# The order of the first loads in a hybrid retention/SSD layer on eight cores

## What is computed

```
mod = silu(cond) @ w_ada + b_ada                 # shift, scale, gate, twice (6 x 1024)
h   = x * (1 + scale1) + shift1
q, k, v, g, z, [xs, B, C], dt = split(h @ w_in)  # 3592 columns
ret = bidirectional retention (4 heads, decay per head, swish gate, RMS norm)
ssd = bidirectional SSD (8 heads; depthwise conv of width 5 and silu on xs, B, C; gated RMS norm)
x   = LN1(ALPHA * x + gate1 * (concat(ret, ssd) @ w_out))
x   = LN2(ALPHA * x + gate2 * SwiGLU(x * (1 + scale2) + shift2))
```

## Time and profile before

| what | value |
|---|---|
| median of 3 runs | 834.82 us (832.24 to 897.93) |
| the profiled execution, its own time | 834.51 us |
| its span, first to last instruction, core 0 | 833.5 us (the 8 cores: 825.6 to 833.5) |
| TensorE matmul busy in the span | 706.9 us, 85% |
| DVE, ACT, POOL busy | 49%, 40%, 35% |
| mean granted TensorE clock, core 0 | 0.938 |

### The profile page before, as it was taken

How to read it: one execution, slowest core, us unless ns; L and a number is a source line. 1 busy time by engine, 2 the same in 40 slices (tenths; PEclk the granted TensorE clock), 3 DMA queues, 4 the chain that set the end, 5 groups by cost and what they waited for, 6 DMA issues and landing times.

```text
span 833.5 us, 12875 instructions; the slowest of 8 cores (825.6 to 833.5 us)
## 1 busy us (share of the span) xinstructions
PE 706.9 (85%) x4414; PEld 371.5 (45%) x4414; DVE 410.9 (49%) x655; ACT 334.9 (40%) x580; POOL 294.9 (35%) x239
## 2 busy tenths in 40 slices
PE   0335999999999986987958399999999999999991
PEld 0333455655565543545425144444444444444440
DVE  0223322544689999487797831112222221466574
ACT  0322334638765333668667261211111111234533
POOL 2012100036655736434945655020000000254555
PEclk9957999989999999998978699999999999999996
DMA  8999400607546376570100937187443336011111
GB/s 181 229 202 159 77 1 11 105 8 118 91 63 105 39 127 142 176 159 20 51 0 26 138 64 101 16 103 87 52 51 50 51 52 152 27 50 74 53 51 76
DMA packets 62431, 69.57 MB, mean 83 GB/s; under 512 B 6144, under 2 KB 52768, under 8 KB 62240
## 3 DMA queue, kind: packets, MB, share of 16 engines
q0 software_dynamic: 47920, 40.72, 35.3%
q1 hardware_dynamic: 14448, 28.03, 10.5%
HBM read 101.05 MB, written 8.40 MB: 131 GB/s over the span
## 4 chain that ended last, share of the span: by engine, by line
PE 69%; DVE 10%; DMA 9%; issue 8%; ACT 3%; POOL 1%; DVEq 0%; ACTq 0%; POOLq 0%
PE psum L450 68%; DVE arena L484 6%; DMA arena<-w_in 4%; DMA arena<-w_ada 4%; DVE arena L495 3%; ACT arena L464 3%; PE psum L515 1%; POOL arena L484 1%; DVE arena L491 1%; ACT L464 1%; DVE arena L499 0%; DVEq L329 0%; DVE arena L505 0%; POOL arena L509 0%; ACTq L329 0%
## 5 line engine op out<-in xcount | busy, mean ns | idle before, releaser
L450 PE MATMUL psum<-arena 128*128 128x512 bf16 (+6 forms) x4208 | 678.5, 320 | 91.0 <-DMA arena<-w_ada 48.7
L450 PEld LDWEIGHTS psum<-arena 128*128 128x128 bf16 (+2 forms) x4208 | 344.5, 101 | 418.8 <-issue 120.1
L484 POOL TENSOR_TENSOR arena<-arena 128x1024 f32<-128x1024 f32 (+3 forms) x156 | 239.9, 1555 | 223.9 <-ACT arena L464 136.7
L464 ACT ACTIVATE arena<-psum 128x512 bf16<-128x512 f32 (+1 forms) x200 | 114.5, 596 | 260.3 <-PE psum L450 244.7
L464 ACT ACTIVATE arena<-arena 128x1 f32<-128x1 f32 (+8 forms) x232 | 144.3, 639 | 150.3 <-DVE arena L495 87.8
L484 DVE TENSOR_TENSOR arena<-arena,psum 128x512 bf16<-128x512 bf16 (+2 forms) x126 | 91.9, 736 | 200.1 <-PE psum L450 178.0
L484 DVE TENSOR_TENSOR arena<-psum,arena 128x512 f32<-128x512 f32 (+3 forms) x174 | 109.3, 649 | 51.0 <-PE psum L450 43.8
L495 DVE SCALAR_TENSOR_TENSOR arena<-arena 128x512 f32<-128x512 f32 (+2 forms) x84 | 95.5, 1160 | 12.2 <-ACT arena L464 11.7
L464 ACT ACT_TABLE_LOAD x32 | 41.1, 1283 | 45.5 <-PE psum L450 24.5
L484 DVE TENSOR_TENSOR arena<-arena 128x1 f32<-128x1 f32 (+8 forms) x74 | 53.5, 730 | 9.3 <-ACT arena L464 5.6
L464 ACT ACTIVATE arena<-psum,arena 128x512 bf16<-128x512 f32 (+1 forms) x56 | 39.3, 717 | 36.0 <-PE psum L450 30.8
(11 more groups left out here) (14 smaller groups left out, 38.6 us busy)
## 6 DMA issues: line engine op xcount, KB each, us to landing
arena<-w_ada POOLq DMA_DIRECT2D x12, 1024.0 KB, 18.0
arena<-x SPq DMA_DIRECT2D x6, 1024.0 KB, 12.4
arena<-w_in POOLq DMA_DIRECT2D x6, 1024.0 KB, 14.4
arena<-x SPq DMA_DIRECT2D x12, 512.0 KB, 4.6
arena<-w_gate POOLq DMA_DIRECT2D x11, 512.0 KB, 7.7
arena<-w_up POOLq DMA_DIRECT2D x11, 512.0 KB, 8.6
y<-arena SPq DMA_DIRECT2D x11, 512.0 KB, 2.6
arena<-w_down POOLq DMA_DIRECT2D x5, 1024.0 KB, 10.4
```

The source lines that it names most:

```text
L450: return P.op(PE, lambda e: e.matmul(out, lhsT=lhsT, rhs=rhs, start=start, stop=stop), [lhsT, rhs], [out], c)
L464: return P.op(ACT, lambda e: e.activation(out=out, in_=in_, func=func, **kw), [in_] + [v_ for v_ in (bias, scale) if isap(v_)], [out] + ([ ...
L484: return P.op(veng(eng), lambda e: e.tensor_tensor(out=out, in0=in0, in1=in1, op=op), [in0, in1], [out], vcost(eng, out, [in0, in1]))
```

## The change

It orders the loads of the start anew. The four small constants (`cols`, the identity block, `smalls`, `tailpos`) get a priority above all else, so SP issues them ahead of x chunk 0. x chunks 1 and 2 no longer wait for the third and the fourth issued `w_ada` slot, but all four halves for the landing of `wBC`. `wxs` waits for the first half of chunk 2, and `tpos`, `cos_t` and `sin_t` wait for `wxs`. No operation is added or taken away.

```diff
+    P.prio = 1e4
     dma(SP, cols[:], cols_d[:, :], "c2")
     dma(SP, V(0, 384, F32), cf_d[:, 0:384], "c0")
     dma(SP, smalls[:], bcast_row(R_SMALL, 48), "c3")
     dma(SP, tailpos[:], cf_d[:, CF_TAIL:CF_TAIL + 2], "c7")
+    P.prio = 0.0
...
     wa = [(ft0, mod_load(ft0)) for ft0 in (0, 8, 4, 12)]
-    wa_ops = [o for o in P.ops if o.is_dma and o.eng == POOL]
     dma(POOL, V(1536, 256, BF16), cb_d[:, 0:256], "c1")
-    x_load(1, 0, after=wa_ops[2:3])
-    x_load(1, 1, after=wa_ops[2:3])
-    x_load(2, 0, after=wa_ops[3:4])
-    x_load(2, 1, after=wa_ops[3:4])
...
     wBC = w_slot(w_in_d, 3072, 520)
+    bc_op = P.ops[-1]
+    xl = [x_load(ck, half, after=[bc_op]) for ck in (1, 2) for half in range(2)]
...
-        dma(SP, tpos, cf_d[:, CF_DELTA:CF_DELTA + 384], "tpos")
+        dma(SP, tpos, cf_d[:, CF_DELTA:CF_DELTA + 384], "tpos", after=[xs_op])
...
-    wxs = w_slot(w_in_d, 2560)
+    wxs = w_slot(w_in_d, 2560, after=[xl[2]])
+    xs_op = P.ops[-1]
...
-    dma(SP, cos_t, cf_d[:, CF_COS:CF_COS + 1024], "c4")
-    dma(SP, sin_t, cf_d[:, CF_SIN:CF_SIN + 1024], "c5")
+    dma(SP, cos_t, cf_d[:, CF_COS:CF_COS + 1024], "c4", after=[xs_op])
+    dma(SP, sin_t, cf_d[:, CF_SIN:CF_SIN + 1024], "c5", after=[xs_op])
```

## The result

| | before | after |
|---|---|---|
| median of the runs, same chip | 833.97 us | 842.85 us |
| the profiled execution, its own time | 834.51 us | 842.82 us |
| its span | 833.5 us (core 0) | 841.8 us (core 2) |
| spans of the 8 cores | 825.6 to 833.5 us | 836.2 to 841.8 us |
| mean granted TensorE clock of the core shown | 0.938 | 0.933 |

The ratio is 1.0112 (95% interval 1.0085 to 1.014): 9 us slower, where 14 were forecast.

The account below looks back on a forecast made before the run. The prediction took the start, up to TensorE's dense stretch, to bound the kernel. It added 10.8 us for the stop, 2.5 for the clock and 0.7 for table loads, 14.0 in all, to 834.51: 848.5 us, range 838 to 856.

Parts of the forecast that it names:

- Small constants: 0: Start loads: small constants ahead of x chunk 0 don't reach the path, since TensorE first waits for a `w_ada` slot.
- `wBC` at 48.5 (47.5 to 50): POOL's queue: the B/C/dt weights land at 48.5 us, 28 us earlier than before.
- x last at 73.7, projections from 76.9: SP's queue and TensorE: late x takes back the 28 us gain; projections begin at 76.9 against 76.98.
- The stop: 10.8 of shift: First Silu on ACT: Exp waiting for late `tpos` hold it until 99.1, against 88.3 before; TensorE waits 10.6 us.
- the first way: Landing of `wxs`: summed from x's 18 us, the remaining bytes at 0.15 MB/us and 1 us for landing, 90.2.
- The clock: 2.5: TensorE after its stop: 13 matmuls at half speed, 2.5 us more, bounds 0 and 3.5.
- The other table loads: 0.7: ACT between Silu: eight more table loads mostly fit, costing TensorE 0.7 us, bounds 0 and 10.3.
- Rival (c): ACT between Silu: the table loads aren't hidden and add up, 858 us; chance 0.14.
- the stretches from 150 us on as before, 14 us later: Rest of the kernel: from 150 us everything runs as before, only 14 us later.
- (a): First Silu on ACT: the Exp don't hold ACT, `wxs` lands by 81.4, only x counts, 834 to 838; chance 0.11.
- (b): Start loads: early `wxs` and quick x make it faster, 831.5, or 830 with `wBC` at 47; chance 0.04.
- (d): TensorE at its stop: the clock stays up or data comes otherwise, 845 to 846; inside the range, no separate chance.

Follow-up runs that it names:

- const_first: Kernel before with only the four small constants issued ahead of x chunk 0, lists made anew; 835.72 us, ratio 0.9992.
- tpos_nowait: Changed kernel, same lists on every engine, only the wait of `tpos` for `wxs` left out; 838.09 us, ratio 1.0046.
- both_same_order: Changed kernel, same lists, without the waits of x chunks 1 and 2 for `wBC` and of `tpos` for `wxs`; 824.06 us, ratio 0.9872.
- wbc_first: Kernel before with `wBC` ahead of `wz` on POOL's queue, lists of TensorE, ACT and DVE kept; ratio 0.9878.
- both_early: Changed kernel without the waits of x chunks 1 and 2 for `wBC` and of `tpos` for `wxs`, scheduled anew; 820.36 us, ratio 0.9822.
- x_early_resched: Changed kernel with x chunks 1 and 2 issued at once, `tpos` still behind `wxs`, lists made anew; 819.83 us, ratio 0.9818.

## Why the prediction was right, and where its sum was off

The mechanism came as predicted: x takes back what `wBC` gains, ACT waits for `tpos` ahead of the first Silu, TensorE stops for ACT. Point by point:

**Small constants: 0.** Right; const_first alone is 0.9992.

**`wBC` at 48.5 (47.5 to 50).** It landed at 49.90, inside the bounds. The working was a little off: SP's queue was not empty at 16 us, it moved 1.70 MB from 2 to 16 and 0.68 after that, and POOL's queue had moved 0.85 MB by then, not 0.61.

**x last at 73.7, projections from 76.9.** The last piece was there at 75.98, inside the bounds (70.7 to 76.5); the projections began at 80.56. Of these 3.7 us 2.3 are the landing, most of it `wBC`'s 1.4. The rest is the transposes: those behind the last landing took 4.6 us, not 3.2, since the granted clock was 0.50 from 77.30 to 80.70, after TensorE had waited 3.00 for the piece: the 14 transposes at 77.55 took 3.22 us where 14 took 1.72 before. And I compared with core 0 of before, 76.98, a late one; the median of the cores is 75.6. Alone the late x is a loss of 3.8 us and not 0: that is tpos_nowait's 1.0046. In the change it is hidden behind the wait for `tpos`.

**The stop: 10.8 of shift.** Measured at the same Silu: 96.63 - 88.27 = 8.4. The step that failed is the landing of the two loads and one table load. `wxs` landed 2.0 earlier than the 92.2 that I chose between 90.2 and 92.3: the first way, by the rate of a full queue, gave 90.2. Its terms, put to the queues (packets, MB, share of 16 engines; from 50 to 76 us, while x runs, and from 76 to 90):

```profile
q0 software_dynamic: 1487, 2.16, 56.5%
q1 hardware_dynamic: 1088, 4.19, 48.0%
...
q0 software_dynamic: 1722, 1.73, 89.9%
```

For the 25 us of x that sum has 18 at a quarter of x's rate and 7 alone at 0.15, together 2.1 MB on q0, which is right. Behind x it leaves 2.3 MB at 0.15 MB/us; there were 1.73 at 0.12. The two misses nearly cancel, so the exact hit is in part luck. `tpos` took 3.62 from issue, not 3.2. The estimate of 2.5 us that the prediction works out from the Trainium skill (DMA: Bandwidth & Descriptors, Anatomy of one DMA) was further off; that section gives its figures for transfers that GpSimd issues, and this load is issued by SP. And I counted a load of the Exp table ahead of the Exp, 1.28, that wasn't needed; before's own timeline has none ahead of its Exp at 34.88, only one at 20.84. 2.0 - 0.4 + 1.3 less 0.4 of small steps is the 2.5 us from 99.1 to 96.63. TensorE's stop is shorter still, 6.69 for 10.6, since with 80.56 for 76.9 it also began later.

**The clock: 2.5.** The windows of TensorE, after (length, busy (matmuls), granted clock, DMA share, GB/s; answers to the earlier trace rows):

```profile
77.30:80.70 3.40, 3.15 (x15) 0.50 1.17 169
80.70:94.40 13.70, 9.39 (x45) 1.00 0.70 119
94.40:96.77 2.37, 0.00 (x0) 0.50 0.65 263
96.77:101.20 4.43, 4.43 (x16) 0.50 0.00 0
101.20:120.00 18.80, 18.80 (x93) 1.00 0.00 1
```

After the stop it is 0.50 for 4.43 us, which costs half of that, 2.2. The half clock of before at the first projections is not paid again there (they run at 1.00 from 80.70), but it is paid by the transposes of 77.30 to 80.70 instead.

**The other table loads: 0.7.** Nothing. Two runs with TensorE at a granted 1.00 all the way show it: the tenth Silu on core 5 of both_same_order, with the eight loads ahead of it, and of wbc_first, with none of the eight:

```profile
98.71 0.69 ACT L464 ACTIVATE arena<-psum,arena 128x512 bf16<-128x512 f32 x1 [0.84 <-PE psum L450]
...
100.24 0.69 ACT L464 ACTIVATE arena<-psum,arena 128x512 bf16<-128x512 f32 x1 [0.84 <-PE psum L450]
```

From the first projection it is 98.71 - 66.22 = 32.49 us in the one and 100.24 - 67.75 = 32.49 in the other. In the change the shift grew by 1.7, from 8.4 at the first Silu to 10.1 at the tenth (111.99 in before, 122.12 after), no more than the 2.2 of the clock. ACT had room, but not much: 16.19 us busy of the 19.23 from 96.77 to 116.00, where I had leaned on 3.76 of 10. The prediction's 12.2 us of ACT for the eight loads and seven Exp add up to 12.1, and its ten table loads were nine, without the one ahead of the first Exp. The Trainium skill (ScalarE: Activation LUTs, What ACT_TABLE_LOAD costs) adds 1.38 us of drain to each load; in ACT's timeline the next instruction follows at 94.65 + 1.28 = 95.93, so there was none here. Rival (c) didn't come, with the drain or without it.

**What came back later.** The forecast had the stretches from 150 us on as before, 14 us later. The shift is 10.5 at the 148.71 of before (159.19 after) and 8.9 at 180.78 (189.64). Between them lies a stretch at half clock (windows of TensorE, columns as above), in before:

```profile
163.84:174.08 10.24, 10.24 (x40) 0.51 0.00 0
```

and in after:

```profile
176.30:183.10 6.80, 6.80 (x22) 0.50 0.00 0
```

It is 3.4 us shorter after, worth half, 1.7. What makes it longer or shorter wasn't tried. So 8.4 + 2.2 - 1.7, less some 0.6 of differences between lines, is the 8.3 by which the profiled times differ. They are of a late core of before and a middle one of after, so 8.3 is less than the 9.4 of the ratio. Of the 5.7 us between forecast and result, 2.4 are the landing and the table load, 0.3 the clock after the stop, 0.7 the loads, 1.7 the later clock, and some 0.6 are spread thin.

Of the rivals, (a), that the Exp don't hold ACT, is what tpos_nowait makes: 838.09 for a forecast of 834 to 838. (b), faster, needed `wxs` before 81; it was at 90.18. (d), the clock stays up, didn't happen.

## What to carry to other kernels

When loads are put in a new order, write down for each one that is moved back who reads it first and what stands behind that reader in its engine's list: 0.4 us of Exp with a late input held a Silu and through it the matmuls. Put the weights that the first dense stretch needs first in their queue, as wbc_first does (0.9878). Small constants may go ahead of everything; alone that neither cost nor gained here (const_first, 0.9992). A link of `after=` cost nothing here where the DMA engines stayed full and no reader stood waiting for its load (x to `wxs`); it cost 5.5 us where one did (`wxs` to `tpos`). And test two suspected waits in all four combinations, since each hides the other.

## What the runs showed that was not expected

The change rests on the view that x beside the `w_ada` slots keeps the weights back. It does, and it pays nevertheless; that was expected of both_early, but not yet of the change when the prediction was made. The two queues of both_early between 20 and 35 us (packets, MB, share of 16 engines):

```profile
q1 hardware_dynamic: 848, 3.26, 65.8%
q0 software_dynamic: 848, 0.86, 40.3%
```

The same number of packets, and nearly four times the bytes for SP's queue. The Trainium skill (DMA: Bandwidth & Descriptors, Queues, rings and completion order) says that each DMA engine goes around its queues packet by packet, and the trace agrees, 848 and 848. In the change the queues share alike from 60 to 71 us (634 packets and 2.45 MB to 627 and 0.64), but not from 50 to 60, where POOL's queue is still at the rest of `cstS` (it landed at 59.0): 285 and 1.12 MB to 384 and 1.05. So beside the slots x takes its 4 to 1 early or late. Early, the last `w_ada` slot comes at 56 (55.80 in x_early_resched), but then POOL's queue has the engines alone, and `wBC` is there at 62.6 (26.49 + 36.1), before the transposes end at 64.5. Held behind `wBC`, x runs while TensorE has nothing else to do.

The second surprise is what a stop in TensorE costs behind its end: 2.2 us after the stop in the change, 2.5 at the first projections of before, and nothing in wbc_first, both_same_order and both_early, where transposes run into projections without a stop.
